# Two program lanes of an attention stage get a step more: the compressed keys' second layer, and the latent values by token tile

## The reference, cut to what matters

```python
# _nsa_group: eight heads, two key heads; three kinds of attention are summed by gates
kc = _compress(_rope(k_cmp...), cmp_pe[0], cmp_w1[0], cmp_b1[0], cmp_w2[0], cmp_b2[0])
vc = _compress(v_cmp..., cmp_pe[1], cmp_w1[1], cmp_b1[1], cmp_w2[1], cmp_b2[1])
p_c = _masked_softmax(einsum('bsgrd,bgnd->bgrsn', qg, kc) * scale, mask_c)
o_cmp = einsum('bgrsn,bgnd->bsgrd', p_c, vc)
# ... selected blocks (o_s) and a window (o_w)
o = gt[:, :, 0] * o_cmp + gt[:, :, 1] * o_s + gt[:, :, 2] * o_w

def _compress(k, pe, w1, b1, w2, b2):      # 15 blocks of 32 tokens
    hid = jax.nn.gelu(flat @ w1 + b1)      # first layer, 2048 -> 128
    return hid @ w2 + b2                   # second layer, 128 -> 64

# _dsa_group: eight heads over a latent of 128; an indexer picks 64 keys for each query
score = einsum('bths,bth->bts', relu(logits), wi_b);  _, idx = lax.top_k(score, 64)
o = einsum('bshr,hrd->bshd', o_lat, w_uv)  # the kernel multiplies the latent by w_uv first
```

## Time and profile before

| | us |
|---|---|
| median of 3 runs | 1389.52 |
| lowest and highest run | 1388.03, 1398.24 |
| profiled execution, its own time | 1398.37 |
| its span | 1396.4 |
| attention stage of the first block, about | 112 to 246 |

### The profile page before, as it was taken

How to read it: one execution, slowest core, us unless ns; L and a number is a source line. 1 busy time by engine, 2 the same in 40 slices (tenths; PEclk the granted TensorE clock), 3 DMA queues, 4 the chain that set the end, 5 groups by cost and what they waited for, 6 DMA issues and landing times.

```text
span 1396.4 us, 12873 instructions
## 1 busy us (share of the span) xinstructions
PE 1013.8 (73%) x5366; PEld 582.4 (42%) x5366; DVE 529.5 (38%) x983; ACT 289.3 (21%) x457; POOL 28.7 (2%) x42
## 2 busy tenths in 40 slices
PE   1787888799879998899986855665555555555674
PEld 0676767686566786677764211111100111111120
DVE  6976666775543498577665100000000000000002
ACT  3322343552331333551321000000000000000000
POOL 0010000100000001000000000000000000000000
PEclk9997789999999999899996988667877877778687
DMA  9895211576434468232266999999999999999994
GB/s 390 321 369 224 91 65 59 218 284 268 174 118 151 151 248 337 76 129 103 102 251 272 421 429 431 430 432 430 430 429 432 430 429 431 430 432 430 429 432 182
DMA packets 41001, 415.13 MB, mean 297 GB/s; under 512 B 4912, under 2 KB 4912, under 8 KB 7792
## 3 DMA queue, kind: packets, MB, share of 16 engines
q1 hardware_dynamic: 38160, 405.75, 71.1%
q10 hardware_dynamic: 2784, 8.57, 1.7%
HBM read 413.26 MB, written 1.05 MB: 297 GB/s over the span
## 4 chain that ended last, share of the span: by engine, by line
PE 41%; DMA 39%; DVE 14%; ACT 4%; issue 2%; POOL 1%; DVEq 0%; POOLq 0%; ACTq 0%
DMA ring<-in_w_egu 12%; DMA ring<-in_w_ed 10%; DMA arena<-in_w_ed 7%; DMA arena<-in_w_egu 7%; PE PS L633 7%; PE PS L634 7%; PE PS L635 7%; PE PS L1234 4%; PE PS L932 3%; DVE ringR L1434 3%; PE PS L555 2%; PE PS L1296 2%; DVE arena L1311 2%; DMA ring<-in_w_in 1%; ACT ringR L2328 1%
## 5 line engine op out<-in xcount | busy, mean ns | idle before, releaser
L1234 PE MATMUL PS<-ring,arena 128*32 128x512 f32 (+1 forms) x1152 | 173.6, 738 | 107.7 <-DMA ring<-in_w_egu 107.7
L633 PE MATMUL PS<-ringR,arenaR 128*128 128x512 f32 (+1 forms) x520 | 217.4, 418 | 31.6 <-DVE arenaR L1422 24.1
L634 PE MATMUL PS<-ringR,arenaR 128*128 128x512 f32 (+1 forms) x520 | 209.8, 403 | 0.0
L635 PE MATMUL PS<-ringR,arenaR 128*128 128x512 f32 (+1 forms) x520 | 209.4, 403 | 0.0
L1434 DVE TENSOR_TENSOR ringR<-ring,ringR 128x2048 fp32r<-128x2048 f32 (+1 forms) x66 | 148.7, 2255 | 108.9 <-ACT ringR L2328 103.9
L1311 DVE SCALAR_TENSOR_TENSOR arena<-arena,PS 128x256 f32<-128x256 f32 (+2 forms) x68 | 33.3, 498 | 376.3 <-ACT arena L2745 366.5
L2328 ACT ACTIVATE ringR<-ring 128x2048 fp32r<-128x2048 f32 (+1 forms) x66 | 123.8, 1884 | 90.9 <-PE PS L635 61.5
L1234 PEld LDWEIGHTS PS<-ring,arena 128*32 128x32 f32 x1152 | 36.2, 129 | 235.4 <-DMA ring<-in_w_egu 171.2
L1296 PE MATMUL PS<-ring,arena 128*32 128x512 f32 x512 | 88.1, 823 | 53.4 <-DMA ring<-in_w_ed 52.8
L633 PEld LDWEIGHTS PS<-ringR,arenaR 128*128 128x128 f32 x520 | 101.2, 195 | 60.0 <-DVE arenaR L1422 31.0
L555 PE MATMUL PS<-CT,arena 128*128 128x128 f32 (+1 forms) x352 | 65.5, 336 | 79.5 <-DVE arena L1311 27.9
(11 more groups left out here) (328 smaller groups left out, 866.3 us busy)
## 6 DMA issues: line engine op xcount, KB each, us to landing
ring<-in_w_egu SPq DMA_DIRECT2D x48, 2048.0 KB, 35.6
ring<-in_w_ed SPq DMA_DIRECT2D x32, 2048.0 KB, 34.4
ring<-in_w_vad SPq DMA_DIRECT2D x40, 1024.0 KB, 6.9
ring<-in_w_egu SPq DMA_DIRECT2D x24, 1536.0 KB, 30.0
arena<-in_w_egu SPq DMA_DIRECT2D x16, 2048.0 KB, 35.6
arena<-in_w_ed SPq DMA_DIRECT2D x12, 2048.0 KB, 32.5
ring<-in_w_in SPq DMA_DIRECT2D x22, 1024.0 KB, 4.8
ring<-in_w_gu SPq DMA_DIRECT2D x22, 1024.0 KB, 4.8
```

What stands on the lines that cost most here:

```text
L633: mm(o, xh(k, t), hi[:, c], start=k == 0, stop=False)
L634: mm(o, xh(k, t), s.viewr[:, c], start=False, stop=False)
L635: i = mm(o, xl(k, t), hi[:, c], start=False, stop=k == nk - 1)
L1234: i = mm(PS[32 * ee:32 * ee + 32, b + a_, 0:fw], XEv[:, k, grp, 32 * ee:32 * ee + 32], wv[:, ee, a_, :], start=k == 0, stop=k == 7, tile_p ...
```

## The change

Four edits in the generators, the same on every engine that the lane has:

- lane c gets one more yield in front of its second layer. On TensorE and ScalarE turn 5 is then empty; on VectorE turn 5 is `hidden(1)` alone, and the wait for L822 and the copies behind it come in turn 6. All later steps of the lane fall one turn later, up to turn 15.
- lane d gives each token tile of the latent values a step of its own: tile 0's product and its copy in turn 7, tile 1's product and ScalarE's copy in turn 8.
- the counts in `schedules` follow: 8 steps for d, 15 for c, and the needs that name them.
- lane o's third step needs all 15 steps of c: it falls in turn 15, and the halves of `out1` behind it in turns 16 to 19 (19 holds only lane o).

No instruction is added or taken away, and no DMA moves in the order of loads.

```diff
-    n = {"p": 3, "f": 16, "0": 18, "1": 18, "i": 24, "d": 7, "c": 14, "o": 7}
+    n = {"p": 3, "f": 16, "0": 18, "1": 18, "i": 24, "d": 8, "c": 15, "o": 7}
...
-            needs[h, 12 + 3 * t] = [("d", 7), ("i", 12 * (t + 1))]
+            needs[h, 12 + 3 * t] = [("d", 8), ("i", 12 * (t + 1))]
     for t in range(2):
-        needs["c", 9 + 4 * t] = [("0", 3 * t + 3), ("1", 3 * t + 3)]
+        needs["c", 10 + 4 * t] = [("0", 3 * t + 3), ("1", 3 * t + 3)]
...
-    needs["o", 2] = [("0", 12), ("1", 12), ("c", 14), ("i", 21)]
+    needs["o", 2] = [("0", 12), ("1", 12), ("c", 15), ("i", 21)]
...
@@ tensor, prepare_d
                     mm(PS[:, 6, :], CKT[:, 128 * t:128 * t + 128], PR("wuv"), start=True, stop=True).then_inc(*sig("pe d vu", t))
-                yield
+                    yield
@@ scalar, prepare_d
-                for _ in range(4):
+                for _ in range(5):
                     yield
```

## The result

The changed kernel takes **1402.52 us** (median of 15 runs, 1395.82 to 1414.54). The kernel before, run beside it on the same chip, takes 1397.17 (15 runs, 1388.03 to 1398.24). The ratio is 1.0051, with a 95% interval of 1.0036 to 1.0066: slower by half a per cent, where 0.1% faster was forecast. The predicted 1388.3 is 14.2 us off. Of that, 7.7 are the base (the three runs shown ahead had a median of 1389.52, the fifteen have 1397.17), 1.2 are the gain that did not come, and 5.3 are a loss where the forecast had a gain.

The account below looks back on a forecast made before the run. Prediction: in attention no engine is full, they wait for each other in turn; the kernel's end is memory-bound. 4.7 us gained by pass 3, 4.2 by pass 4, 1.2 at the end: 1389.52 becomes 1388.3 us; range 1382 to 1398.

Parts of the forecast that it names:

- Turn 5: Keys' second layer: TensorE's 4.46 us wait goes, lane d's pair ends at 160.4 for 163.98, 3.6 us gained.
- turns 6 and 7: VectorE runs without a gap from L1524 to the latent copy L1671, ending at 175.6 for 179.48, 3.9 us gained.
- the latent tiles: The weight's half no longer waits for the latent copy: L1434 starts at 178.7; adds 0.6, making 4.5 us gained.
- turns 8 and 9: Lane c's delayed subtraction: L746 starts at 183.2 for 188.02; 4.7 us carried to pass 3's first maximum, 192.9 for 197.56.
- The new wait at L2469: ScalarE's exponential (L2465 in the forecast) would newly wait for lane c's subtraction, which stands behind L1434 on VectorE.
- Turns 10 to 13: Pass 3 to pass 4: VectorE is the bound for 19.65 us; pass 4 at 213.0, 4.2 us gained.
- the forecast's 244.3: Start of the other half's first transposes, for 245.49 before: 222.6 + 20.7 + 1.0, 1.2 us gained.
- The end, where it is given back: Behind pass 4: the later output projection no longer hides pass 4's tail, turning 4.2 us of gain into 1.2.
- 223.3 or later: When lane o's eight transposes end with most at half clock; 221.8 at full clock, 222.6 taken.
- Rival 2: Slower: a TensorE hole before turn 9 keeps half clock through pass 3's keys; 2.5 us lost, 1392.0 us; chance 0.2.
- The two signs given for rival 2: Gain at pass 3's first maximum under about 3.5 us; first transposes of the other half over 247.

Follow-up runs that it names:

- Kernel 6: Kernel before plus a blank lane c step behind the first token tile's output, so only turns 11 to 15 get the changed order; 1404.08 us, ratio 1.0062.
- Kernel 4: Changed kernel plus four extra 128x240 matmuls, output overwritten, in TensorE's waits in turn 11; 1395.22 us, ratio 0.9991.
- kernel 3: Kernel before with only lane o's third step held back to turn 15; 1398.41 us, ratio 1.0002.
- kernel 5: Changed kernel plus 2 and 6 extra matmuls of 16 columns in the two waits of turn 11; 1402.69 us, ratio 1.0043.
- kernel 7: Kernel before plus four extra matmuls of 240 columns (1 and 3) in turn 11; 1396.25 us, ratio 0.9996.
- kernel 8: Kernel before plus lane d's step for each token tile and four extra matmuls of 240 columns in turn 11; 1402.43 us, ratio 1.0034.
- kernel 1: Kernel before with lane d's edit alone, a step for each token tile, lane c as it was; 1402.93 us, ratio 1.0042.
- kernel 9: Kernel before with both second-layer products of lane c in turn 6 and lane d's step for each token tile; 1395.41 us, ratio 0.9987.
- kernel 11: kernel 9 plus four extra matmuls of 240 columns in turn 11; 1391.22 us, ratio 0.9963.
- kernel 12: kernel 11 plus four more extra matmuls of 240 columns in TensorE's wait in turn 13; 1399.37 us, ratio 1.0008.

## Why the prediction was wrong

- **Turn 5, turns 6 and 7, the latent tiles, turns 8 and 9: right.** 160.9 for 160.4, 176.1 for 175.6, 179.09 for 178.7, 183.57 for 183.2, and 192.79 for 192.9 at pass 3. The new wait at L2469 came as described. That the size fits to 0.1 us is partly luck: the same orders of work gave gains from 0.8 to 4.8 at this place, 2.9 between their means.
- **"Turns 10 to 13": the step that failed first.** It said that VectorE "is the bound, for 19.65 us". The forecast took VectorE's unbroken row as a property of the work, and carried 4.2 of the gain to pass 4. It was unbroken because TensorE ran L746 in 3.79 us, at full clock. At half clock it takes 7.09, TensorE becomes the bound (3.05 of idle at L1603), and the 19.65 become 23.18 where the forecast had 20.1. Pass 4 starts at 215.97. That is 3.0 of the 5.1 us between the forecast's 244.3 and the measured 249.38. The text had named this sign: it is wrong in kind if VectorE shows idle rows between passes 3 and 4.
- **The prediction priced tile 1's scores by their length and not by their place.** It followed the delayed lane into this stretch for VectorE ("puts L1756 ... into this stretch") and did not follow its matmuls L833 from turn 11 to 12. In front of the fall, from 196 to 201, TensorE is busy for 2.53 of 5 us after the change; before it, from 198 to 203, for 4.47, and there the clock fell too, at 204.1, but came back at 207.5. Kernel 6 has this move without the gain in front and loses 4.6 us up to pass 4, 1.0062 in all. Kernel 4 holds the clock with work that computes nothing and has 20.24 there.
- **"The end, where it is given back": right in kind, too small.** The sum gave back 3.0 us behind pass 4; 5.1 are measured, the other 2.1 of the miss. With the clock held in turns 11 and 12 it is still 4.0 (kernel 4). About 1.1 of that is the later output projection (kernel 3). The rest goes with lane c's last product standing behind the transposes, for which VectorE waits 4.66 where it waited 0.40. In the changed kernel L843, L746 and eight transposes also ran at half clock (1.92, 3.51, 1.91), the case that the text had put at "223.3 or later"; they end at 228.2. How the 4.0 divide between order and clock was not separated, since kernel 4 has half clock there too, from 212.0 to 222.3.
- **So even a clock that held would not have made the forecast true.** Kernel 4 has the other half 0.2 later than before, not 1.2 sooner, and its pass 3 came early as well.
- **Rival 2 had the right mechanism in the wrong place.** It let the clock fall in turn 9 and take the keys of pass 3. There the clock came back as before. It fell later, behind the transposes of turn 11, where the rival's "VectorE and not TensorE is the bound right behind" was taken as safe. The two signs given for rival 2 disagree: the other half is over 247, but the gain at pass 3 was not under 3.5.
- **The rule of the Trainium skill.** The prediction weighed the Trainium skill's "TensorE: Matmul & The Clock Gate", section "HAM oscillation — how this bites in real kernels", by which gaps without work drop the array to half clock. The traces agree in part: the gap of turn 5 closed, and 0.80 became 0.85 in that stretch. Kernels 4 and 5 show that it is not all: with equal gaps and equal busy time the clock held behind matmuls of 240 columns and fell behind matmuls of 16. And faster matmuls paid only where VectorE waited for them.
- **The base.** 7.7 of 14.2 us come from three runs whose median was low. The range took the profiled execution's 1398.37 in, but only just, and left no room above it for a loss. The text also said that nothing in attention tells that execution from the others. Three more profiles of the same order up to pass 3 (kernels 3, 6, 7) are 0.8 to 2.6 us earlier there.

**What stays open:** why kernel 8's runs fall into two groups, why the clock falls and rises at other moments in the same order of work up to pass 3 and behind pass 4, and what decides the time behind attention. The granted clock differs in those stages, but no run changed it there alone. What exactly the chip counts when it sets the clock was not measured.

## What to carry to other kernels

When a change moves a block of matmuls from one turn to another, read the granted clock on both sides of its old place and of its new one, and ask what is left in the old place: here a TensorE that waited between a few transposes dropped to half clock, and the small matmuls that followed ran at half without a gap between them. An "unbroken" VectorE row is a bound only at the clock that stood beside it; price the feeding matmuls at half clock too, and see who is late then. And where a fall of the clock is suspected of costing several microseconds, a few wide matmuls of no use in a wait are a cheap test for it. Read the test from a landmark right in front of the fill: two executions of the same order stood up to 2.6 us apart there.

## What the runs showed that was not expected

- The values' product, 32 matmuls of 64 columns, kept TensorE busy for 7.09 us at half clock and did not bring it up; at full clock the same 32 did not let it fall (3.79 in kernel 4). In kernels 1 and 9 half clock ended in the first half microsecond of it, and it took 3.99 and 3.91.
- Matmuls of 16 columns in a gap were no help (1.0043), matmuls of 240 in the same time were (0.9991).
- Kernels 11 and 12 reach the other half 0.3 us apart and end 12.0 apart in their profiles, 8.2 in their medians, with the same code behind. A microsecond of attention is thus less sure at the end than the prediction took from the earlier trace rows.
